# First attention: both parts of the values side by side in one stationary, the sums scaled on VectorE

## The reference, cut to what matters

```python
kb, vb = with_prev(k), with_prev(v)
s = jnp.einsum('bnqkgd,bnskd->bnkgqs', q, kb) * (HD ** -0.5)
...
logits = jnp.where(mask[None, :, None, None], s + bias, NEG)
...
m = jnp.maximum(jnp.max(logits, axis=-1, keepdims=True), sink)
p = jnp.exp(logits - m)
probs = p / (jnp.sum(p, axis=-1, keepdims=True) + jnp.exp(sink - m))
o = jnp.einsum('bnkgqs,bnskd->bnqkgd', probs.astype(vb.dtype), vb)
return o.reshape(B_, T, SWA_HEADS * HD) @ w_o
```

## Time and profile before

| | |
|---|---|
| median of 3 runs | 2140.07 us (2138.89 to 2140.48) |
| profiled execution | 2137.59 us |
| its span | 2135.3 us |
| first attention, pairs 0 to 7 | 62.85 to 252.3 us of the span |
| one pair (1 to 5) | 25.35 us |

### The profile page before, as it was taken

The page is one execution under the profiler, slowest core; times in us unless marked ns, Lnnn a source line. Parts: engine busy times, 40 slices in busy tenths (PEclk is TensorE's granted clock), DMA queues, the critical chain, the costliest instruction groups (busy, mean ns, idle before and its releaser), DMA issues.

```text
span 2135.3 us, 28166 instructions
## 1 busy us (share of the span) xinstructions
PE 2096.7 (98%) x10916; PEld 1765.4 (83%) x10916; DVE 1649.7 (77%) x2603; ACT 1134.4 (53%) x1770; POOL 192.1 (9%) x274
## 2 busy tenths in 40 slices
PE   9999999999999999999999999999999999899997
PEld 7899888888888888888888988888888877688885
DVE  7777658998887997897564264688888866799997
ACT  6777535444444433554432242677777325588885
POOL 0000200000001000000111042000000101111112
PEclk9999999999999999999999999999999999999999
DMA  4122812655559998752453112000001714999997
GB/s 157 50 70 60 296 69 94 210 181 186 183 202 396 395 346 304 230 200 43 148 178 108 46 50 86 10 1 1 1 11 48 293 50 182 345 383 384 384 384 251
DMA packets 114998, 374.55 MB, mean 175 GB/s; under 512 B 13440, under 2 KB 13728, under 8 KB 113200
## 3 DMA queue, kind: packets, MB, share of 16 engines
q1 hardware_dynamic: 86544, 273.00, 34.9%
q0 software_dynamic: 27168, 95.56, 13.5%
q10 hardware_dynamic: 1152, 4.19, 0.5%
HBM read 303.48 MB, written 69.21 MB: 175 GB/s over the span
## 4 chain that ended last, share of the span: by engine, by line
PE 88%; DVE 7%; ACT 3%; DMA 1%; issue 1%; POOLq 0%; SPq 0%; POOL 0%; ACTq 0%
PE psum L99 26%; PE psum L100 26%; PE psum L101 26%; PE psum L3310 3%; PE psum L3323 2%; PE psum L1072 1%; ACT MP_hi L3407 1%; DVE small L3452 1%; DVE MP_lo L3497 1%; PE psum L1041 1%; ACT PB L3379 1%; PE psum L4346 1%; DVE idx L3968 1%; DVE w_lo L286 1%; DVE cur L3971 1%; DVE vals L3966 1%
## 5 line engine op out<-in xcount | busy, mean ns | idle before, releaser
L277 ACT ACTIVATE w_hi<-rawe 128x1024 fp32r<-128x1024 f32 x210 | 216.5, 1056 | 149.1 <-DVE rawe L1797 71.9
L99 PE MATMUL psum<-U_hi,w_hi 128*128 128x512 f32 x688 | 273.0, 397 | 0.5 <-DVE U_lo L560 0.3
L286 DVE TENSOR_TENSOR w_lo<-rawe,w_hi 128x1024 fp32r<-128x1024 f32 x210 | 248.5, 1221 | 31.5 <-ACT w_hi L277 30.8
L100 PE MATMUL psum<-U_lo,w_hi 128*128 128x512 f32 x688 | 268.7, 391 | 0.0
L101 PE MATMUL psum<-U_hi,w_lo 128*128 128x512 f32 x688 | 268.5, 390 | 0.0
L286 DVE TENSOR_TENSOR w_lo<-raw,w_hi 128x1024 fp32r<-128x1024 f32 (+2 forms) x167 | 189.5, 1142 | 81.2 <-ACT w_hi L277 81.1
L277 ACT ACTIVATE w_hi<-raw 128x1024 fp32r<-128x1024 f32 (+3 forms) x168 | 164.3, 984 | 79.0 <-PE psum L101 40.3
L99 PE MATMUL psum<-B_hi,w_hi 128*128 128x512 f32 x448 | 175.5, 392 | 0.9 <-ACT cbuf L1513 0.9
L99 PE MATMUL psum<-w_hi 128*128 128x512 f32 x448 | 175.0, 391 | 0.0
L101 PE MATMUL psum<-B_hi,w_lo 128*128 128x512 f32 x448 | 174.5, 390 | 0.0
L100 PE MATMUL psum<-B_lo,w_hi 128*128 128x512 f32 x448 | 174.5, 389 | 0.0
(11 more groups left out here) (569 smaller groups left out, 5093.0 us busy)
## 6 DMA issues: line engine op xcount, KB each, us to landing
rawe<-in_w_e SPq DMA_DIRECT2D x112, 512.0 KB, 18.0
rawe<-in_w_dn SPq DMA_DIRECT2D x70, 512.0 KB, 6.1
rawx<-in_w_e SPq DMA_DIRECT2D x56, 512.0 KB, 18.6
rawe<-ta SPq DMA_DIRECT2D x43, 512.0 KB, 6.9
ta<-cbuf SPq DMA_DIRECT2D x64, 256.0 KB, 2.5
raw<-in_w_dn SPq DMA_DIRECT2D x26, 512.0 KB, 6.2
ta<-rg SPq DMA_DIRECT2D x48, 256.0 KB, 2.0
raw<-in_w_e SPq DMA_DIRECT2D x24, 512.0 KB, 17.8
```

The source lines that it names most:

```text
L99: e.matmul(o, l[0], r[0], start=first, stop=False, skip_group_check=skip)
L100: e.matmul(o, l[0], r[1], start=False, stop=False, skip_group_check=skip)
L277: act.e.activation(hi, src, ACT.Copy).then_inc(w_hi, 1)
L286: dve.e.tensor_tensor(lo, src, f(hi), ALU.subtract).then_inc(w_lo, 1)
```

## The change

Pairs are now two heads of one group (2j and 2j + 1), so both heads read the same values. `VS` holds v_hi and v_lo of that group side by side, 64 columns each, as one stationary of 128 columns. Two passes (PT_hi and PT_lo as moving operands) give all products: rows 0 to 63 of the bank take v_hi's part, rows 64 to 127 v_lo's (with it a fourth product, lo x lo). A key block has two passes of 512 columns where it is even, four of 256 where it is odd, two of 256 for key block 7; a bank now holds two query blocks of both heads, and there are four such blocks m for each pair. A block is taken out in three pieces: ACT's `low` (L823 after) copies rows 64 to 127 of 512 columns to rows 0 to 63 of a buffer in SBUF; DVE adds them to rows 0 to 63, one add of 64x256 for each head (L922 after, `out`); and for every second block DVE multiplies 128x512 by RB in SBUF (L928 after, `scale`). They run in every odd step. V(0), V(1), V(3) and V(5) wait for the `out` of the block before the last (its bank); before, V(0) and V(3) waited for `out` of the pair before. The splits wait for `scale`. On POOL's queue the bias load of pair j + 3 now stands ahead of the spill of half 0. Bias, sinks and the keys' index follow the new pairs; the zeros in `vz` and their memsets are gone.

```diff
-    vz = pair("vz", [8, 192], O_V + 32 * KB, O_V + 38 * KB)
+    VS = at("VS", [2, 8, P], O_V + 32 * KB, F32R)
+    s_low = [at(f"slow{i}", [512], O_V + (40 + 2 * i) * KB) for i in range(2)]
...
+    def evict_step(j, s):
+
+        return (j - 1, 3) if s == 1 else (j, s // 2 - 1) if s % 2 else None
+
+    O_BLOCKS = [(j, m) for j in range(8) for m in range(4)]
...
-        return src, vz[x][:, 4 * i:4 * i + 4, :].rearrange("p n (a d) -> p n a d", d=64)[:, :, 0:3:2, :]
+        return src, VS[:].rearrange("p h n c -> p n h c")[:, 4 * i:4 * i + 4, :, 64 * x:64 * x + 64]
 
     def turned(j, kb, ap):
 
-        return ap.rearrange("p (h q) -> p h q", h=2)[:, :, 0:256 if kb < 7 else 128]
+        return ap[:, 0:512 if kb < 7 else 256]
...
             raw, hi, _ = out_of(j, i)
-            act.wait_ge(*sw.dve("out", j, i))
+            act.wait_ge(*sw.dve("scale", j, i))
             if 0 < j < 6:
                 act.wait_ge(*spill_out[i].at(2 * j))
             act.e.activation(hi, raw, ACT.Copy).then_inc(*sw.act.one("split", j, i))
+
+        def lower(j, m):
+            act.wait_ge(*sw.pe("times_v", j, 2 * m + 1))
+            if j or m > 1:
+                act.wait_ge(*sw.dve("out", *O_BLOCKS[4 * j + m - 2]))
+            act.e.activation(s_low[m % 2][rows_of(0), :], bank(B_O[m % 2])[rows_of(1), :], ACT.Copy).then_inc(
+                *sw.act.one("low", j, m))
...
+                if evict_step(j, s) in O_BLOCKS:
+                    lower(*evict_step(j, s))
...
-                        act.wait_ge(*sw.dve("out", j - 1, i))
+                        act.wait_ge(*sw.dve("scale", j - 1, i))
...
-        def out(j, i):
-            dve.wait_ge(*sw.pe("times_v", j, 3 + 4 * i))
-            dve.wait_ge(*sw.act("row", j, i))
+        def out(j, m):
+            i, x = m // 2, bank(B_O[m % 2]).rearrange("p (n h q) -> p n h q", n=2, h=2)
+            y = s_low[m % 2][:].rearrange("p (n h q) -> p n h q", n=2, h=2)
+            raw = out_of(j, i)[0][:, 256 * (m % 2):256 * (m % 2) + 256].rearrange("p (n q) -> p n q", n=2)
+            dve.wait_ge(*sw.act("low", j, m))
             if j > 5:
                 dve.wait_ge(*sw.pe("q", 7, 1))
             elif j:
                 dve.wait_ge(*spill_out[i].at(2 * j))
-            dve.e.tensor_tensor(out_of(j, i)[0], bank(B_O[i]), RB[:, half(i)],
-                                ALU.mult).then_inc(*sw.dve.one("out", j, i))
+            for h in range(2):
+                o = dve.e.tensor_tensor(raw[rows_of(h)], x[rows_of(0), :, h, :], y[rows_of(0), :, h, :], ALU.add)
+            o.then_inc(*sw.dve.one("out", j, m))
+            if m % 2:
+                raw = out_of(j, i)[0]
+                dve.wait_ge(*sw.dve("out", j, m))
+                dve.wait_ge(*sw.act("row", j, i))
+                dve.e.tensor_tensor(raw, raw, RB[:, half(i)], ALU.mult).then_inc(*sw.dve.one("scale", j, i))
...
-                if s == 1 and j > 0:
-                    out(j - 1, 1)
+                if evict_step(j, s) in O_BLOCKS:
+                    out(*evict_step(j, s))
                 if s == 3 and j > 0:
                     split(j - 1, 1)
-                if s == 5 and now:
-                    out(j, 0)
...
-                            m = pe.e.transpose(bank(B_T[u % 2], 256 * h + P * i, 256 * h + P * i + P),
+                            m = pe.e.transpose(bank(B_T[u % 2], 256 * i + P * h, 256 * i + P * h + P),
...
-                                                kst[h][x][:, k0:n * P + P], start=x == 0, stop=x == 1)
+                                                kst[(j + 1) // 4][x][:, k0:n * P + P], start=x == 0, stop=x == 1)
...
-        if j and kb == 0:
-            pe.wait_ge(*sw.dve("out", j - 1, 0))
-        if j and kb == 3:
-            pe.wait_ge(*sw.dve("out", j - 1, 1))
-        spans = ((0, 256),) if kb not in (3, 7) else ((0, 128), (128, 256)) if kb == 3 else ((0, 128),)
-        for h in range(2):
-            for c0, c1 in spans:
-                q0 = kb * P + c0
-                o = psum[:, B_O[q0 // 512], q0 % 512:q0 % 512 + c1 - c0]
-                m = mm3(pe.e, o, [vz[x][:, kb, 64 * h:64 * h + 128] for x in range(2)],
-                        [PT[u % 3][x][:, 256 * h + c0:256 * h + c1] for x in range(2)],
-                        (kb, c0, h) in ((0, 0, 0), (3, 128, 0)), (kb, c0, h) in ((3, 0, 1), (7, 0, 1)), True)
-        m.then_inc(*sw.pe.one("times_v", j, kb))
+        if (kb == 0 or kb % 2) and kb < 7:
+            before = 4 * j + (kb + 1) // 2 - 2
+            if before >= 0:
+                pe.wait_ge(*sw.dve("out", *O_BLOCKS[before]))
+        v, p, m = VS[:, j // 4, kb, :], PT[u % 3], kb // 2
+        for x in range(2):
+            if kb % 2 == 0:
+                o = pe.e.matmul(bank(B_O[m % 2]), v, p[x][:], start=(kb, x) == (0, 0), stop=False,
+                                skip_group_check=True)
+                continue
+            o = pe.e.matmul(bank(B_O[m % 2], 256, 512), v, p[x][:, 0:256], start=False, stop=x == 1,
+                            skip_group_check=True)
+            if kb < 7:
+                o = pe.e.matmul(bank(B_O[1 - m % 2], 0, 256), v, p[x][:, 256:512], start=x == 0, stop=False,
+                                skip_group_check=True)
+        o.then_inc(*sw.pe.one("times_v", j, kb))
...
-    c["bias"] = np.ascontiguousarray(np.stack([b[:8], b[8:]], 1).transpose(0, 2, 1, 3))
+    c["bias"] = np.ascontiguousarray(b.reshape(8, 2, 128, 256).transpose(0, 2, 1, 3))
```

More of the change, by code:

```diff
@@ L717, in _program @@
                 sw.dve.plan(("sum", j), ("inverse", j))
[L718 to L719 removed]
+            if evict_step(j, s) in O_BLOCKS:
+                y, m = evict_step(j, s)
+                sw.dve.plan(("out", y, m), *([("scale", y, m // 2)] if m % 2 else []))
             if s == 3 and j > 0:
                 sw.dve.plan(("split", j - 1, 1))
[L722 to L723 removed]
             if s == 7 and now:
@@ L763, in swa_pool @@
             pool.e.dma_start(bS[z][:], A["bias"][z]).then_inc(bias_in[z].sem, 16)
-        for j in range(-1, 6):
-            if j > 0:
+        for j in range(-1, 9):
+            if j == 6:
+                pool.wait_ge(*sw.pe("q", 7, 1))
+                for i in range(2):
+                    pool.wait_ge(*spill_out[i].at(10))
+                for k in range(5):
+                    reload(pool, k)
+            if j == 7:
+                for i in range(2):
+                    pool.wait_ge(*sw.pe("turn", 6, 7))
+                    pool.e.dma_start(X[:, 2 * i:2 * i + 2, :], A["xT"][:, 2 * i:2 * i + 2, :]).then_inc(xr_in[i].sem, 16)
+                for i in range(2):
+                    pool.wait_ge(*spill_out[i].at(12))
+                reload(pool, 5)
+            if 0 < j < 7:
                 pool.wait_ge(*sw.dve("split", j - 1, 1))
                 spill(pool, j - 1, 1)
-            if j >= 0:
-                pool.wait_ge(*sw.dve("split", j, 0))
-                spill(pool, j, 0)
             if j + 3 < 8:
@@ L773, in swa_pool @@
                 pool.e.dma_start(bS[(j + 3) % 2][:], A["bias"][j + 3]).then_inc(bias_in[(j + 3) % 2].sem, 16)
[L774 to L786, removed]
+            if 0 <= j < 6:
+                pool.wait_ge(*sw.dve("split", j, 0))
+                spill(pool, j, 0)
     def spill(pool, j, i):
@@ L878, in swa_act @@
                     act.e.activation(sink_e, sink_e, ACT.Exp).then_inc(*sw.act.one("sink", j + 1))
-    def zeros_beside_v(dve):
-        for x in range(2):
-            dve.e.memset(f(vz[x][:, :, 64:128]), 0.0).then_inc(*sw.dve.one("vz0", x))
     def sinks(dve):
@@ L1086, in swa_pe @@
             hand_over(B_T[i], 1, sw.dve("turn", 7, 6 + i))
-            hand_over(B_O[i], 1, sw.dve("out", 7, i))
+            hand_over(B_O[i], 1, sw.dve("out", 7, 2 + i))
     def times_v(pe, j, kb):
@@ L1147, in _program @@
     for t in T_SO[2:4]:
-        resume_at[t] = [sw.dve("split", 5, 1), spill_out[1].at(12), sw.dve("out", 7, 1), sw.pe("row", 7, 1)]
+        resume_at[t] = [sw.dve("split", 5, 1), spill_out[1].at(12), sw.dve("scale", 7, 1), sw.pe("row", 7, 1)]
     for n in range(8):
@@ L4522, in lay_out @@
         v[:, o:o + a.size // 128] = vec(a)
-    pairs = np.arange(16).reshape(2, 8).T.reshape(-1)
+    pairs = np.arange(16)
     v[:, 96:112] = swa_sinks[0][pairs][None, :]
```

7 lines of the change are left out of this document (3 added, 4 removed).

## The result

The changed kernel takes 2146.76 us, median of 6 runs (2146.28 to 2149.09), against 2139.78 (2138.33 to 2141.54) for the one before: 7.0 us more, ratio 1.0035, 95% interval 1.0022 to 1.0048. The prediction, 2147 and slower, holds. The profiled execution took 2149.09 with a span of 2146.8.

What follows compares the result with a forecast made beforehand. PE's own issue bound pairs 1 to 5; after the change a ring of waits, 26.56 us per pair, would. The terms 6.0 + 2.6 - 2.5 + 1.0 = +7.1 us gave 2147.2 for the median; forecast 2147, range 2139 to 2153.

Steps and rivals of the forecast that it cites:

- What PE saves: V passes on PE: 4.17 us per pair instead of 6.85, so PE needs 22.65 for a pair instead of 25.34.
- What the other two get: Adds and scales bring DVE to 23.1 us per pair, four copies bring ACT to 21.4.
- The ring: Chain of waits from V(1), which now waits for `out`, via V(5) to the next V(1): 26.56 us, against 25.35 before.
- The second part: The ring from V(5) to the next V(1), through PE, ACT and DVE: 12.98 us.
- the first: The ring from V(1) to V(5), through PE, ACT and DVE: 13.58 us.
- PE's stops: PE idles 3.9 us per pair, some 2.3 before V(1) and 1.6 before V(5).
- The sum: Whole kernel: 6.0 + 2.6 - 2.5 + 1.0 = +7.1 us, 2147.2 for the median.
- From pair 5 to 6: V(1) of pair 5 to V(1) of pair 6: 26.2 us instead of 23.6, +2.6 (bounds +1.5 to +3.0).
- From V(1) of pair 6 to the end of V(7) of pair 7: PE saves 5.1 us there; the middle of bounds 0 and -5.1 was taken, -2.5.
- The tail: Behind V(7) of pair 7 the last half's split, 1.2 us early before, comes 1.0 late: +1.0.
- the rival on the clock: Much slower: long PE waits in pair 6 may halve the clock, costing up to half of 10 us, 2152; chance 6%.
- my own list: Signs of being wrong: pair under 25.35, PE waits at V(0) or V(3), no tail wait, clock falls in pairs 1 to 7.

Runs made afterwards that it cites:

- less on DVE beside the ring: Changed kernel without the multiplication by 1/denominator (`scale`, two of 128x512 per pair on DVE): ring 26.60 us.
- more on PE ahead of the waits: Changed kernel with V(0) and V(4) computed four times over, 12 passes of 512 columns more per pair: ratio 1.0044 to the kernel before.
- less on the ring: Changed kernel without ACT's copy `low`, the adds taking zeros in its place: ring 25.54 us.
- the same work in another order: Changed kernel with two q behind PT_lo, adds and scale, copy ahead of r_wide, w_hi and w_lo in steps 2 and 3: 2127.71 us, ring 23.34.
- the copy alone: Changed kernel with only ACT's copy of step 1 moved ahead of r_wide: ring 26.60 us.
- the q alone: Changed kernel with only DVE's two q of steps 1 and 5 moved behind PT_lo, adds and scale: ring 25.91 us.
- both: Changed kernel with DVE's two q behind PT_lo, adds and scale, and ACT's copy of step 1 ahead of r_wide: 2135.72 us, ring 24.77.
- the control: Kernel before the change with two q behind PT_lo and `out`, w_hi and w_lo in steps 2 and 3: 2139.36 us, ratio 1.0001.

## Why the prediction was right

- **What PE saves:** a V takes 0.55 and V(7) 0.32 in the trace, as priced. The window's busy time of 23.33 in pair 3 is 0.7 above my 22.65 because it counts, at each of the three stops, a latency's tail that no next matmul hides; from start to start PE's work is 22.65, as predicted.
- **What the other two get:** the adds take 417 ns (priced 418), the second starts 0.42 behind the first and the next instruction 0.45 behind the second; the copies take 595 (priced 590) and stand 0.02 behind PT_hi. DVE's load is 22.58 (23.1), ACT's 21.24 (21.4). The scale is 693 ns. The Trainium skill's overlap of 0.09 for neighbours on ACT ("ScalarE: Activation LUTs", section "What ACT_TABLE_LOAD costs"), by which the sum would have been 2144.4, holds on one side of the copy and not on the other: 31 of the 32 copies start 0.02 or 0.03 behind the instruction ahead, but behind three of a pair's four the next one overlaps by 0.09 to 0.11 (147.41 against 147.50 above). I had priced a gap on both sides. What the skill says of VectorE ("VectorE: DVE Perf Modes", section "Two Vector instructions with no wait between them") agrees: the first add, whose rows start where PT_lo's do, overlaps it by 0.08, the second, which writes the other half of the rows, doesn't.
- **The ring:** 13.58 and 12.98, in all 26.56, predicted; 13.62, 12.99, 26.61 measured. The second part agrees in every term within 0.07. In the first, three terms are off and cancel. ACT in step 3:

```profile
152.83 0.60 ACT L852 ACTIVATE PT_hi<-psum 128x512 fp32r<-128x512 f32 x1 [1.94 <-PE psum L1056]
153.45 0.60 ACT L823 ACTIVATE slow<-psum 64x512 f32<-64x512 f32 x1
153.95 0.50 ACT L870 ACTIVATE EX<-EX,small 128x256 f32<-128x256 f32 x1
```

  From the end of PT_hi(3) to the first exponential it is 0.52, not 0.65, by the overlap behind the copy; from there to the end of PT_hi(4) 3.17, not 3.08; from the adds' end (161.49 + 0.84) to V(5) 0.15, not 0.05. That the sum meets the measured 13.62 within 0.04 is partly luck.
- **PE's stops:** 3.96 per pair from start to start, against 3.9 predicted. I had 2.3 at V(1) and 1.6 at V(5); they are 1.75 and 1.66, and 0.55 stands in step 0, where the queries' product waits for w_lo, which I had missed. The ring's sum didn't depend on where PE waits.
- **The sum:** V(1) of pair 0 to that of pair 5, 133.10 (202.09 - 68.99) against 5 x 25.35 = 126.75: +6.3, predicted +6.0. From pair 5 to 6: 26.28, +2.7, predicted +2.6. From V(1) of pair 6 to the end of V(7) of pair 7: 259.22 - 228.37 = 30.85 against 252.32 - 219.64 = 32.68, -1.8; predicted -2.5. The tail: +1.25, predicted +1.0. V(1) of pair 0 began 0.3 earlier. At the product behind V(7), k = 7 and i = 1, that is 264.65 - 256.50 = 8.15 in these two executions; the medians differ by 7.0. Behind the attention both kernels do the same, and the difference drifts between 8 and 11.5 us in these two traces, which says how far a single one can be trusted. By the traces the attention alone costs 8.15 where I had 7.1, so the median's agreement within 0.1 us is closer than the terms behind it.
- **The step that was only half right:** the rival on the clock (6%). By my own list a fall of the clock in pairs 1 to 7 was a sign of being wrong, and it came: the granted clock fell in pair 6, where it was 1.00 in the kernel before. Windows of 2 us around it:

```profile
226.00:228.00 2.00, 0.00 (x0) 0.00 (x0) 0.79 (x3) 1.95 (x4) 2.00 (x5) 0.64 1.01 309
228.00:230.00 2.00, 1.63 (x8) 1.66 (x9) 1.72 (x4) 1.95 (x7) 0.26 (x1) 0.50 1.08 406
230.00:232.00 2.00, 2.00 (x11) 2.00 (x11) 1.27 (x2) 2.00 (x7) 0.00 (x0) 0.50 1.06 399
232.00:234.00 2.00, 2.00 (x12) 1.80 (x11) 1.80 (x10) 0.99 (x3) 0.00 (x0) 0.65 1.10 412
```

  PE stood 3.18 us ahead of V(1) and then ran at 1.2 GHz for some 5 us. With V(0) and V(4) computed four times the wait there was 1.80 and the clock stayed at 1.00 in all of pair 6, and V(1) to V(5) of that pair took 11.00 us instead of 11.83, though it held six passes more. So the fall costs at least 0.8 up to there. It may be the 0.7 by which pairs 6 and 7 gave back less than predicted; that isn't shown. I had priced it at up to 5.

The mechanism, adds and copies of a step ahead of V(1) and V(5) in queues that are one chain, is shown by four runs: less on DVE beside the ring changes nothing, more on PE ahead of the waits changes nothing, less on the ring pays at once, and the same work in another order takes 3.3 us per pair off. What I had drawn too narrowly is the ring's cause: I called it V(1)'s new wait for `out`. Without that wait (copy and adds a step earlier) the ring is as long, 26.9.

## What to carry to other kernels

When an engine that bound is relieved, ask what the next ring is before asking what the next load is: here three loads of 21 to 23 us stood in a ring of 26.6. Follow that ring through whole in-order queues, and move behind the contested instruction what its consumer doesn't need; where two queues end together at one handover, moving one pays only the distance to the other (here 0.00 for the copy alone and 0.70 for the q alone, against 1.84 for both). And keep the control: the order that is worth some 19 us to the changed kernel is worth nothing to the one before.
